# Dense projections with [rounded, remainder] activations as one moving operand of 512 columns, in a hybrid SSD, attention and expert layer on one Trainium2 core

## What is computed

```python
u = rms_norm(h, norm_mix_g)
proj = u @ w_in                       # z 1024, xbc 2048, dt 16, q, k, v 1024 each, f 8, gates 2048
xbc = silu(causal_depthwise_conv(xbc, conv_w, conv_b))      # 4 taps, 2048 channels
y_ssd = ssd scan of xbc with dt, 16 heads; times silu(z); rms_norm by group
s = q @ k.T * scale + c[query] - c[key]; causal mask; y_fox = softmax(s) @ v      # 8 heads
gates = sigmoid(gate_logit + b_gates)
merged = gates[0] * (y_ssd @ w_ssd_branch) + gates[1] * (y_fox @ w_fox_branch)
h = h + merged @ w_out
h = h + cross_attention(rms_norm(h), rms_norm(mem))         # w_cross_q, w_cross_kv, w_cross_o, 4 heads
h = h + moe_ffn(rms_norm(h), router, experts)               # 32 experts, 4 per token
out = rms_norm(h, norm_final_g)
```

## Time and profile before

| | |
|---|---|
| median of three executions | 1374.87 us (1374.8 to 1377.45) |
| profiled execution | 1377.79 us, of which the span is 1375.8 us |
| TensorE matmul busy | 1308.2 us, 95% of the span, 7442 instructions |
| TensorE weight load | 727.4 us, 53% |
| VectorE | 427.3 us, 31% |
| ScalarE | 362.4 us, 26% |
| GpSimd | 33.9 us, 2% |
| DMA | 471.33 MB, mean 343 GB/s |
| granted TensorE clock | 0.993 on average |

### The profile page before, as it was taken

How to read it: one execution, slowest core, us unless ns; L and a number is a source line. 1 busy time by engine, 2 the same in 40 slices (tenths; PEclk the granted TensorE clock), 3 DMA queues, 4 the chain that set the end, 5 groups by cost and what they waited for, 6 DMA issues and landing times.

```text
span 1375.8 us, 17463 instructions
## 1 busy us (share of the span) xinstructions
PE 1308.2 (95%) x7442; PEld 727.4 (53%) x7442; DVE 427.3 (31%) x810; ACT 362.4 (26%) x559; POOL 33.9 (2%) x57
## 2 busy tenths in 40 slices
PE   6999999999999999999999999999899998889997
PEld 6999999999999433333333333333233333233332
DVE  6765667576553211211121112111112111112111
ACT  5854455654433211111111111111111111111102
POOL 2001200001001000000000000000000000000000
PEclk9999999999999999999999999999999999999999
DMA  7555444359848899999999999999999999999995
GB/s 235 158 152 152 137 143 123 127 182 334 283 147 318 352 376 428 427 417 427 428 427 427 429 427 427 427 429 428 427 428 426 429 427 428 427 428 429 425 428 232
DMA packets 97680, 471.33 MB, mean 343 GB/s; under 512 B 8349, under 2 KB 69929, under 8 KB 71625
## 3 DMA queue, kind: packets, MB, share of 16 engines
q1 hardware_dynamic: 97376, 470.19, 85.2%
q10 hardware_dynamic: 232, 0.07, 0.0%
HBM read 469.19 MB, written 1.05 MB: 342 GB/s over the span
## 4 chain that ended last, share of the span: by engine, by line
PE 64%; DMA 34%; ACT 1%; DVE 1%; issue 0%; DVEq 0%; SPq 0%; ACTq 0%
DMA arena<-in_w_expert_in 30%; PE ps L914 15%; PE ps L956 9%; PE ps L567 7%; PE ps L568 7%; PE ps L569 7%; DMA arena<-in_w_expert_out 3%; PE ps L883 3%; PE ps L867 3%; PE ps L558 1%; PE ps L560 1%; PE ps L559 1%; PE ps L875 1%; PE ps L891 1%; PE ps L939 1%; PE ps L933 1%
## 5 line engine op out<-in xcount | busy, mean ns | idle before, releaser
L914 PE MATMUL ps<-arena 128*64 128x512 f32 x2048 | 455.6, 596 | 44.3 <-DMA arena<-in_w_expert_in 42.6
L914 PEld LDWEIGHTS ps<-arena 128*64 128x64 f32 x2048 | 143.9, 137 | 348.5 <-issue 262.8
L1712 DVE TENSOR_SCALAR arena<-ps 128x512 f32<-128x512 f32 x32 | 22.1, 692 | 677.4 <-PE ps L914 677.4
L956 PE MATMUL ps<-arena 128*64 128x512 f32 x1024 | 227.0, 595 | 0.6 <-DMA arena<-in_w_expert_out 0.6
L567 PE MATMUL ps<-A_hi,w_hi 128*128 128x256 f32 x576 | 166.5, 289 | 5.8 <-DVE A_lo L1336 4.5
L568 PE MATMUL ps<-A_lo,w_hi 128*128 128x256 f32 x576 | 163.5, 284 | 0.0
L569 PE MATMUL ps<-A_hi,w_lo 128*128 128x256 f32 x576 | 163.4, 284 | 0.0
L1369 DVE TENSOR_TENSOR w_lo<-w_raw,w_hi 128x1024 fp32r<-128x1024 f32 x120 | 142.8, 1231 | 59.6 <-ACT w_hi L1053 59.1
L956 PEld LDWEIGHTS ps<-arena 128*64 128x64 f32 x1024 | 70.7, 137 | 137.0 <-issue 135.5
L1274 ACT ACTIVATE arena<-arena 128x512 f32<-128x512 f32 x32 | 20.1, 629 | 450.7 <-DVE arena L1712 450.7
L1053 ACT ACTIVATE w_hi<-w_raw 128x1024 fp32r<-128x1024 f32 x120 | 119.9, 1048 | 25.3 <-DMA w_raw<-in_w_out 7.8
(11 more groups left out here) (301 smaller groups left out, 1341.0 us busy)
## 6 DMA issues: line engine op xcount, KB each, us to landing
arena<-in_w_expert_in SPq DMA_DIRECT2D x120, 2048.0 KB, 46.2
arena<-in_w_expert_out SPq DMA_DIRECT2D x61, 2048.0 KB, 43.6
w_raw<-in_w_in SPq DMA_DIRECT2D x32, 1024.0 KB, 5.5
arena<-in_w_expert_in SPq DMA_DIRECT2D x16, 1024.0 KB, 9.4
w_raw<-in_w_cross_kv SPq DMA_DIRECT2D x8, 1024.0 KB, 7.5
arena<-in_w_expert_out SPq DMA_DIRECT2D x6, 1024.0 KB, 8.6
w_raw<-in_w_ssd_branch SPq DMA_DIRECT2D x4, 1024.0 KB, 5.1
w_raw<-in_w_fox_branch SPq DMA_DIRECT2D x4, 1024.0 KB, 5.1
```

The costliest lines, as they stand in the source:

```text
L914: last = mm(ps[64 * half:64 * (half + 1), b, :], xg_cols[:, 2 * (s % 2) + c, s // 2, :], w[:, at:at + 512], start=False, stop=(s == 3 and ...
L956: last = mm(ps[64 * half:64 * (half + 1), 3, :], at_cols[:, c, s - 4, :], w[:, at:at + 512], start=(s == 4 and c == 0), stop=(s == 5 and c ...
L1712: V_.tensor_scalar(glu, ps[:, 0, :], LIMIT, None, ALU.min).then_inc(glu_ready, 1)
```

## The change

1. Hi and lo of an activation (A, B, C) and of the weights now lie side by side in one tile, so that one matmul moves 512 columns: hi weight x [hi, lo] activation into a whole bank, then lo weight x hi activation, 256 columns, onto the second half of the bank. By token: hi activation x [lo, hi] weight, then lo activation x hi weight onto the first half. Each half of a unit has its own bank, three go round (BANKS = 3), and a half waits for the half three before.
2. VectorE drains every half and adds the two sums: a reduction over pairs that lie 256 columns apart (out and co: two additions into hT). ScalarE's silu, scaling and bias follow in place, in SBUF, after VectorE's drain. The gates of ssd and fox are separate operations (`gated_ssd`, `gated_fox`).
3. The last convolution tap goes to GpSimd: a multiply into `ctmp` and an addition.
4. The running sums of the second branch's scores are added by TensorE into the score's bank, with a negative identity (`ident_m`); `negc` goes.
5. In the z units, VectorE's order is changed (z 0 drained after the last taps, the memory norm after z 2's remainders).
6. Routing: logits go to bank 3, one filler matmul is added at each of three places, the wait for the item count goes behind expert 15. At the end, gather, transposes and bias for items that don't exist go into the branch for more than 32 items.

```diff
-    ON_ACT = {"xbc", "z", "q", "gate", "cq"}
+    ON_ACT = {"z", "q", "gate", "cq"}
...
-    PJ = 3
+    BANKS = 3
...
+        w_both = rounded("w_both", 10, [P, 2, 4, KT, P])
+        w_lo, w_hi = w_both[:, 0], w_both[:, 1]
...
+            both = rounded(f"{name}_both", first, [P, 2, KT, S])
+            splits[name] = (both[:, 0], both[:, 1], both)
...
+            for c in range(16):
+                pool.wait_ge(dve_drained, c + 1)
+                link(nc.gpsimd.tensor_scalar(ctmp[c % 2], xb[:, c, 4:4 + S], prm[:, CW + 48 + c:CW + 49 + c], None, ALU.mult))
+                pool.wait_ge(conv_half, c + 1)
+                nc.gpsimd.tensor_tensor(xc[:, c, :], xc[:, c, :], ctmp[c % 2], ALU.add).then_inc(conved, 1)
...
                 for j in range(2):
-                    o = ps[:, u % PJ, j * 256:(j + 1) * 256]
+                    g = 2 * u + j
+                    if g >= BANKS:
+                        pe.wait_ge(dve_drained, g - BANKS + 1)
+                    o = ps[:, g % BANKS, :]
                     if name in BY_TOKEN:
...
-                            mm(o, a_hi[:, k, rows], wh, start=(k == 0), stop=False)
-                            mm(o, a_hi[:, k, rows], wl, start=False, stop=False)
-                            last = mm(o, a_lo[:, k, rows], wh, start=False, stop=(k == KT - 1))
+                            mm(o, a_hi[:, k, rows], w_both[:, :, slots, k, :], start=(k == 0), stop=False)
+                            last = mm(o[:, 0:256], act[1][:, k, rows], w_hi[:, slots, k, :], start=False, stop=(k == KT - 1))
                     else:
...
-                            mm(o, w_hi[:, s, k, :], a_hi[:, k, :], start=(k == 0), stop=False)
-                            mm(o, w_hi[:, s, k, :], a_lo[:, k, :], start=False, stop=False)
-                            last = mm(o, w_lo[:, s, k, :], a_hi[:, k, :], start=False, stop=(k == KT - 1))
+                            mm(o, w_hi[:, g % 4, k, :], a_both[:, :, k, :], start=(k == 0), stop=False)
+                            last = mm(o[:, S:2 * S], w_lo[:, g % 4, k, :], a_hi[:, k, :], start=False, stop=(k == KT - 1))
...
             def scores(h):
-                running_sum(4, SSD_H + h)
...
+                for part in range(2):
+                    mm(ps[:, b, 0:P], row, acT[part][:, 0:P], start=False, stop=(part == 1), skip_group_check=True)
+                    last = mm(ps[:, b, P:384], row, acT[part][:, :], start=False, stop=(part == 1), skip_group_check=True)
...
+            keep_clock(0, 1)
...
+            keep_clock(2, 1)
...
+            keep_clock(1, 1)
...
-            pe.wait_ge(meta_ready, 1)
-            n_items = pe.value_load(meta[0:1, NI:NI + 1], min_val=NE, max_val=MAX_ITEMS)
...
(ScalarE)
-                act.wait_ge(w_done, 2 * u + 2)
-                bank = ps[:, u % PJ, :]
-                two = bank.rearrange("p (a b) -> p a b", a=2)
+                act.wait_ge(dve_drained, drained(u))
+                pair = slice(2 * n, 2 * n + 2)
+                if name == "z":
+                    ins = A(zs[:, pair, :], zs[:, pair, :], ACT.Silu)
...
(VectorE)
+                for j in range(2):
+                    g, c = 2 * u + j, 2 * n + j
+                    dve.wait_ge(w_done, 2 * u + 2 if name in BY_TOKEN else g + 1)
+                    bank = ps[:, g % BANKS, :]
+                    if name in ("out", "co"):
+                        link(V_.tensor_tensor(hT[:, c, :], hT[:, c, :], bank[:, 0:S], ALU.add))
+                        V_.tensor_tensor(hT[:, c, :], hT[:, c, :], bank[:, S:2 * S], ALU.add).then_inc(dve_drained, 1)
+                        continue
...
+                    V_.tensor_reduce(to, bank.rearrange("p (h t) -> p t h", h=2), AX.X, ALU.add).then_inc(dve_drained, 1)
+            def gated_ssd(n):
...
+                V_.tensor_tensor(merged[:, pair, :], merged[:, pair, :], gate[:, pair, :], ALU.mult).then_inc(merge_ssd, 1)
+            def gated_fox(n):
...
+                link(V_.tensor_tensor(mtmp[:, pair, :], mtmp[:, pair, :], gate[:, 8 + 2 * n:10 + 2 * n, :], ALU.mult))
+                V_.tensor_tensor(merged[:, pair, :], merged[:, pair, :], mtmp[:, pair, :], ALU.add).then_inc(merge_made, 1)
...
-                for tap in range(1, 4):
+                for tap in (1, 2):
...
-            step("z", 0)
+            split_weights(unit("z", 1))
             conv(7)
...
-            apply_norm(1, muT, muT, G_MEM)
+            drain("z", 0)
...
-            step("z", 1)
+            split_weights(unit("z", 2))
+            apply_norm(1, muT, muT, G_MEM)
+            drain("z", 1)
```

More of the change, by code:

```diff
@@ L82, in drained, with finished @@
     def drained(u):
-        act = units[u][0] in ON_ACT
-        return act, sum((units[v][0] in ON_ACT) == act for v in range(u + 1))
+        return 2 * u + 2
+    def finished(u):
+        return sum(units[v][0] in ON_ACT for v in range(u + 1))
     SPLIT = {"u": 0, "yssd": 4, "mu": 8, "merged": 12, "u2": 16}
@@ L129, in layer_program @@
         xdt = tiles(page(9), TB)
+        ctmp = [page(7, 256, 256 * j) for j in range(2)]
         qT, kT, V = tiles(page(0), KT), tiles(page(1), KT), tiles(page(7), TB)
@@ L144, in layer_program @@
         raw_w = [w_raw[:, j, :, :] for j in range(2)]
-        w_hi = rounded("w_hi", 12, [P, 4, KT, P])
-        w_lo = rounded("w_lo", 10, [P, 4, KT, P])
+        w_both = rounded("w_both", 10, [P, 2, 4, KT, P])
+        w_lo, w_hi = w_both[:, 0], w_both[:, 1]
         splits = {}
         for name, first in (("A", 16), ("B", 18), ("C", 8)):
-            splits[name] = [rounded(f"{name}_{part}", first + j, [P, KT, S]) for j, part in enumerate(("hi", "lo"))]
+            both = rounded(f"{name}_both", first, [P, 2, KT, S])
+            splits[name] = (both[:, 0], both[:, 1], both)
         A_, B_, C_ = splits["A"], splits["B"], splits["C"]
@@ L526, in mean_squares @@
                         last = mm(ps[:, 3, 508 + tb:509 + tb], sq[:, c, tb * P:(tb + 1) * P], c_d[:, 0:1],
-                                  start=(c == 0 and tb == 0), stop=(c == KT - 1), skip_group_check=True)
+                                  start=(c == 0 and tb == 0 and not opened), stop=(c == KT - 1), skip_group_check=True)
                 last.then_inc(ms_psum, 1)
@@ L764, in _ @@
                 if h >= 1:
-                    pe.wait_ge(dve_drained, drained(unit("cv", y))[1])
+                    pe.wait_ge(dve_drained, drained(unit("cv", y)))
                     pe.wait_ge(xpt_copied, y + 1)
@@ L795, in pair @@
             def pair(n):
-                pe.wait_ge(dve_drained, drained(unit("co", n))[1])
+                pe.wait_ge(dve_drained, drained(unit("co", n)))
                 if n == 1:
@@ L809, in _ @@
             pair(1)
-            project("co", 3, A_)
-            pair(2)
-            pe.wait_ge(dve_drained, drained(unit("co", 3))[1])
-            logits(3).then_inc(lg_psum, 1)
-            mean_squares(squared, 4, 2)
-            by_token(6)
-            by_token(7)
             def keep_clock(bank, n):
@@ L821, in keep_clock @@
                     mm(ps[:, bank, 0:S], idn, tri[:, 0:S], start=True, stop=True)
+            project("co", 3, A_)
+            pair(2)
+            keep_clock(0, 1)
+            pe.wait_ge(dve_drained, drained(unit("co", 3)))
+            logits(3).then_inc(lg_psum, 1)
+            mean_squares(squared, 4, 2, opened=True)
+            by_token(6)
+            by_token(7)
             keep_clock(2, 4)
@@ L1120, in _ @@
                     root(1)
-                act.wait_ge(act_drained, n + 1)
+                act.wait_ge(dve_drained, drained(unit("xbc", n)))
                 for c in (2 * n, 2 * n + 1):
@@ L1184, in _ @@
                 if h == 7:
-                    act.wait_ge(act_drained, drained(unit("gate", 7))[1])
+                    act.wait_ge(act_drained, finished(unit("gate", 7)))
                     gate_sigmoid(0)
@@ L1201, in pair_square @@
             def pair_square(name, n):
-                act.wait_ge(dve_drained, drained(unit(name, n))[1])
+                act.wait_ge(dve_drained, drained(unit(name, n)))
                 A(sq[:, 2 * n:2 * n + 2, :], hT[:, 2 * n:2 * n + 2, :], ACT.Square).then_inc(squared, 1)
@@ new lines, in gated_ssd @@
+            def gated_ssd(n):
+                pair = slice(2 * n, 2 * n + 2)
+                dve.wait_ge(dve_drained, drained(unit("ssd", n)))
+                V_.tensor_tensor(merged[:, pair, :], merged[:, pair, :], gate[:, pair, :], ALU.mult).then_inc(merge_ssd, 1)
+            def gated_fox(n):
+                pair = slice(2 * n, 2 * n + 2)
+                dve.wait_ge(dve_drained, drained(unit("fox", n)))
+                dve.wait_ge(merge_ssd, n + 1)
+                link(V_.tensor_tensor(mtmp[:, pair, :], mtmp[:, pair, :], gate[:, 8 + 2 * n:10 + 2 * n, :], ALU.mult))
+                V_.tensor_tensor(merged[:, pair, :], merged[:, pair, :], mtmp[:, pair, :], ALU.add).then_inc(merge_made, 1)
@@ L1423, in conv @@
                         else:
```

(6 more changed lines are left out.)

131 lines of the change are left out of this document (55 added, 76 removed).

## The result

The changed kernel took 1381.31 us (median of six, 1379.88 to 1382.44), the kernel before 1376.23 us in the same session (1374.8 to 1377.69): ratio 1.0033, 95% interval 1.0022 to 1.0043. It is **slower by 0.33%**, where 1366 us and faster had been forecast; the range held the time. The profiled execution took 1381.41 us, its span is 1379.5 us, 3.7 more than the span of before. The executions of the kernel before lie in two groups, near 1375 and near 1378 us (three and three here, and in changing shares later: 6 and 18, 9 and 14, 5 and 12, 1 and 14), so its median alone moves by up to 3 us from one session to the next.

What follows compares the result with a forecast made beforehand. TensorE bounds the dense part, the DMA stream the expert part. 21.1 us saved less 16.6 of stalls, with routing -3.5 and tail -0.5, sum to -8.5: 1369.3 profiled, 1366 us for a median; range 1352 to 1386.

Steps and rivals of the forecast that it cites:

- So it streams for about 0.216 ... Pair 0.336 ... 23.0 us less: Dense matmuls: a 512- plus a 256-column matmul takes 0.336 us instead of 0.36, over 960 pairs 23.0 us less.
- The stalls of 16.6: Dense part: TensorE waits on VectorE and ScalarE loops cost 16.6 us, leaving the dense part 4.5 us shorter.
- The SSD loop of 21.2 us: SSD units: VectorE and ScalarE loop takes 21.2 us against TensorE's 19.9; after 2.6 us of slack, +2.6.
- The reduction at 0.69: VectorE draining: each half's reduction of 512 PSUM elements to 256 takes 0.69 us, 1.2 us a unit.
- rival 2: VectorE drains: the reduction across the stride costs 1.04 us and VectorE becomes the bound; 1385 us, chance 0.20.
- GpSimd at 0.74 to 0.9 for the multiplication: Last convolution tap: GpSimd's multiply takes 0.74 to 0.9 us, 3.0 to 3.3 per unit with adds, so GpSimd keeps up.
- The clash that I put at 0.6 a unit: Convolution units: GpSimd's operations slow VectorE's remainder pairs, 0.6 us a unit, making the loop 7.1.
- lies in the loop's shadow: Convolution units: moving the last tap takes 2 x 0.41 us off VectorE but does not shorten the loop.
- The marks: Signs to check: dense part ending near 434.5 us, wrong after 442; clock 0.9 or more between 440 and 460.
- The scores, +1.9: Scores of the eight heads: four small rounded matmuls in place of two, 1.9 us more.
- Routing -3.5, tail -0.5: Routing: fillers, chunks and item-count wait give -3.5 us if the clock holds; dropped work for absent last items gives -0.5.
- Rival 3: Dense matmuls: the pair takes 0.36 us, the 23.0 are gone, stalls fall to about 8; 1381 us, chance 0.08.

Runs made afterwards that it cites:

- Experiment 2: Changed kernel with the 256-column matmul of the remainder weights made 512 columns in by-weight units: 1453.75 us (one execution).
- experiment 5: Changed kernel with ScalarE rounding unit n+2's weights before waiting for VectorE's reduction of unit n in the convolution units: 1374.33 us, ratio 0.9979.
- 6: Changed kernel with ScalarE rounding unit n+2's weights before waiting for the merge of unit n in the four fox units: 1377.24 us, ratio 1.0004.
- experiment 4: Changed kernel with the last (fourth) convolution tap moved back from GpSimd to VectorE: 1380.26 us, ratio 1.0024.
- Experiment 10: Kernel before with the weights rounded earlier in the convolution and fox units: 1374.09 us, ratio 0.9982.
- experiment 1: Changed kernel with each activation tile's rounded and remainder halves side by side, so by-weight 512 columns are one contiguous read: 1381.5 us, ratio 1.0032.
- experiment 8: Changed kernel with earlier rounding in convolution and fox units, late copies and expert-bias remainders moved, last tap's multiplication on ScalarE: 1369.4 us, ratio 0.9943.
- experiment 9: Kernel before with only the edits behind the dense part (logits bank, extra clock-keeping matmuls, later item-count wait, trimmed last items): 1375.79 us, ratio 0.9985.

## Why the prediction was wrong

The forecast difference was -8.5 us, the spans of the profiled executions differ by +3.7: 12.2 to explain. By the steps:

- **"So it streams for about 0.216 ... Pair 0.336 ... 23.0 us less": this step failed.** The pair is 0.347 to 0.353. I had the difference of two durations, 0.11 to 0.12 for 256 columns, and put 0.216, twice 0.108, below even its lower edge. That leaves the 512-column matmul a fixed cost of 3 ns, while the 256-column one beside it had 13 in the very rows I quoted. Experiment 2 shows 13 for both. The saving per pair is 7 to 13 ns instead of 24, and the 60 units became only 6.8 shorter instead of 23.0: +16.2. Of this the fixed cost is 10.2 (960 x 10.7 ns), the slower pace of 38 units another 4.1, whose cause stays open, and the rest mostly first matmuls behind a wait. The Trainium skill (TensorE: Matmul & The Clock Gate, Back-to-back issue gap) gives columns by 2.4 GHz plus 2.5 ns for a matmul by itself, 0.216 for 512; here, with rounded f32 operands and new weights for each, the runs show 0.2265, and the measurement decides.
- **The stalls of 16.6 were about right.** They were 13.9 with the two half-clock stretches (2.8) that I had not named, 11.1 without: -2.7. By place: convolution and z 9.4 forecast, 5.8 measured plus 1.4 of clock; SSD 2.6 forecast, none measured; fox and out 3.7 forecast, 4.6 measured; the norm and the second branch 0.9 forecast, none measured; ahead of gate0 0.9 that I had not forecast. The mechanism was as told: a loop of 6.81 us against my 7.1 in the convolution units, 6.66 against 6.75 in the fox units (whose terms, as I wrote them, add up to 6.5), and experiments 5 and 6, which break the two loops, give 7.0 (3.0 of it clock) and 4.1 back. The SSD loop of 21.2 us never showed: three units with what lies between take TensorE 20.55 us, not the forecast 19.9, so four such groups would use up just the 2.6 of slack. Whether the loop itself is 21.2 was not measured.
- **The reduction at 0.69** was right at 0.682, and rival 2 is false. The Trainium skill (Vector Engine (DVE) Microarchitecture Reference, 5.2) told of one read alternating between two regions at full rate; the runs agree, with both regions in PSUM.
- **GpSimd at 0.74 to 0.9 for the multiplication** was wrong: 0.93 where it begins ahead of VectorE's remainders, 1.9 where it begins among them, 1.43 in the mean. It kept up nevertheless. The clash that I put at 0.6 a unit was 0.5 (2.89 against 2.36).
- **The tap on GpSimd "lies in the loop's shadow"** was right: experiment 4.
- **The marks.** I had called it wrong if the dense part ended after 442; it ended at 448. The clock from 440 to 460 was to be 0.9 or more and was 1.00. The scores, +1.9, were 1.8.
- **Routing -3.5, tail -0.5** were -4.8 and -0.4; the clock held, as "if the clock holds" had it. Experiment 10's trace has full clock from 443 to 449 us without these edits, so how much of the 4.8 is theirs is open.
- **The base.** I took 2.9 us off for the place of the profiled execution against the first three runs' median. Later medians of the kernel before were 1376.2 to 1377.9, so that correction was worth 1.6 at most.

Sum: 16.2 - 2.7 - 1.3 + 0.1 - 0.1 = 12.2. Rival 3 (the pair takes 0.36, 1381) gave the measured time at a chance of 0.08, and that is luck: it had nothing saved and stalls of 8, where the runs have 6.8 saved and 13.9 of stalls. The pair lies between it and the forecast, nearer to it in most units. It deserved more: I had named 0.36 as a bound and had no row of the pair, so the largest term of the sum (23.0) was the least measured one.

## What to carry to other kernels

Where a matmul is made longer to save another, price it as columns over the clock plus the fixed cost that the existing matmuls' start-to-start distance shows, not from durations. Take this as the best case: it gives 0.3465 a pair and 13 us saved, and the runs had 6.8. And when a bank's drain moves from one engine to another, look for work that now waits for the drain ahead of work that does not: here rounding the next weights stood behind the wait, and moving that one call in two places, and three small copies with it, turned a loss of 4 us into a gain of 7.5. Not all of that is the idea's: the edits behind the dense part give the kernel before 1.7 without it, and about 3 us of what the moved calls gave back was clock. Put the feeding of the bound engine first in each helper's queue, and repair the stalls before judging the idea.

## What the runs showed of the hardware

- A matmul of rounded f32 operands with fresh 128x128 weights costs its columns plus 13 ns at full clock, for 256 and 512 columns alike in a row of one size (steps of 0.120 and 0.2265 us). Of the two in turn a pair costs 0.347 or 0.353 us; whether the moving operand is one piece or two made no difference (experiment 1).
- TensorE's granted clock fell to its lower level (1.2 GHz) behind a wait of 2.7 us (z1) and behind 3.6 us of matmuls of one column (gate1), in which TensorE is booked as fully busy. Each cost 1.4 us in the changed kernel, and 3.1 in the kernel of experiment 8, where it was down for 6.8 us (191.0 to 197.8) instead of 3.4. The same weak stretch ahead of gate1 passes at full clock in the kernel before and in experiment 5, and not in 9 and 10, whose work there is that of the kernel before, 1.2 us later and 1.5 earlier. It follows that a difference of 2 to 4 us between two kernels can be clock alone (experiment 9), and that a profile of each is needed to tell. What exactly decides stays open.
- GpSimd's 128x256 multiplication of f32 by a column takes 0.93 us where it begins ahead of VectorE's remainders and 1.89 where it begins among them, and a remainder pair goes from 2.36 to 2.89: both lose.
